# Two hybrid blocks on one core: eight more products on constants in the second block's layer norms, and the decay gate's four products in four row groups

## The reference, cut to what matters

```python
for l in range(DEPTH):                                   # DEPTH = 2
    y = hybrid_mixer(x, positions, w_in[l], gla_w_gate[l], gla_b_gate[l], ...)
    x = layer_norm(DN_ALPHA * x + y, ln1_g[l], ln1_b[l])
    y = conv_ffn(x, w_up[l], conv_w[l], conv_b[l], w_down[l])
    x = layer_norm(DN_ALPHA * x + y, ln2_g[l], ln2_b[l])
```

```python
gate_logits = g_lr @ gla_w_gate + gla_b_gate             # [512, 16] @ [16, 512] + [512]
log_a = jax.nn.log_sigmoid(gate_logits.astype(F32)) / GLA_TAU
```

## Time and profile before

| | us |
|---|---|
| median of 3 runs | 3383.66 |
| lowest, highest | 3381.45, 3383.67 |
| the profiled execution's own time | 3377.7 |
| its span, first to last instruction | 3375.9 |
| TensorE busy in it | 3314.1 (98%) |
| DVE, ACT, POOL busy | 1539.0, 1370.6, 1460.8 |

### The profile page before, as it was taken

The page is one execution under the profiler, slowest core; times in us unless marked ns, Lnnn a source line. Parts: engine busy times, 40 slices in busy tenths (PEclk is TensorE's granted clock), DMA queues, the critical chain, the costliest instruction groups (busy, mean ns, idle before and its releaser), DMA issues. The chain is left out here.

```text
span 3375.9 us, 45275 instructions
## 1 busy us (share of the span) xinstructions
PE 3314.1 (98%) x16644; PEld 2745.6 (81%) x16644; DVE 1539.0 (46%) x2470; ACT 1370.6 (41%) x1976; POOL 1460.8 (43%) x1100
## 2 busy tenths in 40 slices
PE   8999999999999999999999999999989999999998
PEld 6888888887788888887778878888878788788887
DVE  5523232225614442225872446544488524464445
ACT  4534232223635342223364453433444734343333
POOL 4434444444333544444433345445544333444443
PEclk9999999999999999999999999999999999999999
DMA  4222222222222222222212222222222121222221
GB/s 142 84 75 77 98 98 90 99 100 95 81 76 75 101 99 100 89 98 94 84 63 75 76 80 99 88 99 99 100 76 88 56 83 63 88 87 100 99 100 63
DMA packets 43819, 298.60 MB, mean 88 GB/s; under 512 B 4816, under 2 KB 5456, under 8 KB 8592
## 3 DMA queue, kind: packets, MB, share of 16 engines
q1 hardware_dynamic: 41696, 291.52, 24.3%
q10 hardware_dynamic: 1968, 4.94, 0.5%
HBM read 294.34 MB, written 2.10 MB: 88 GB/s over the span
## 5 line engine op out<-in xcount | busy, mean ns | idle before, releaser
L340 POOL TENSOR_TENSOR w_lo<-w_raw,w_hi 128x512 fp32r<-128x512 f32 x1048 | 1392.1, 1360 | 1857.1 <-ACT w_hi L1181 1857.1
L504 PE MATMUL ps<-x_hi,w_hi 128*128 128x512 f32 (+1 forms) x2448 | 966.2, 395 | 7.2 <-POOL w_lo L340 4.9
L506 PE MATMUL ps<-x_hi,w_lo 128*128 128x512 f32 (+1 forms) x2448 | 952.0, 389 | 0.0
L505 PE MATMUL ps<-x_lo,w_hi 128*128 128x512 f32 (+1 forms) x2448 | 951.1, 389 | 0.0
L1181 ACT ACTIVATE w_hi<-w_raw 128x1024 fp32r<-128x1024 f32 x524 | 523.9, 1049 | 486.9 <-PE ps L506 374.4
L504 PEld LDWEIGHTS ps<-x_hi,w_hi 128*128 128x128 f32 x2448 | 459.7, 188 | 111.5 <-issue 8.9
L506 PEld LDWEIGHTS ps<-x_hi,w_lo 128*128 128x128 f32 x2448 | 459.5, 188 | 96.1
L505 PEld LDWEIGHTS ps<-x_lo,w_hi 128*128 128x128 f32 x2448 | 460.0, 188 | 93.6 <-issue 2.4
L504 PE MATMUL ps<-y_hi,w_hi 128*128 128x512 f32 x1056 | 411.6, 390 | 2.7 <-POOL w_lo L340 1.9
L505 PE MATMUL ps<-y_lo,w_hi 128*128 128x512 f32 x1056 | 410.9, 389 | 0.0
L506 PE MATMUL ps<-y_hi,w_lo 128*128 128x512 f32 x1056 | 410.9, 389 | 0.0
(11 more groups left out here) (255 smaller groups left out, 3866.3 us busy)
## 6 DMA issues: line engine op xcount, KB each, us to landing
w_raw<-stream SPq DMA_DIRECT2D x274, 1024.0 KB, 4.8
x<-x_t SPq DMA_DIRECT2D x4, 512.0 KB, 5.9
rotary<-rot ACTq DMA_DIRECT2D x4, 512.0 KB, 3.6
y_t<-x SPq DMA_DIRECT2D x8, 256.0 KB, 2.0
ct<-consts ACTq DMA_DIRECT2D x2, 770.0 KB, 5.3
arena<-pos ACTq DMA_DIRECT2D x2, 256.0 KB, 2.6
vec<-vectors ACTq DMA_DIRECT2D x4, 116.0 KB, 2.0
ct<-consts ACTq DMA_DIRECT2D x1, 128.0 KB, 3.6
```

Of the source, the lines that this page charges most:

```text
L340: ins = nc.gpsimd.tensor_tensor(low(c)[:, o:o + S], RAW[:, c % 2, o:o + S], high(c)[:, o:o + S].bitcast(F32), ALU.subtract)
L504: pe.matmul(ps, wh, xh, start=(k == 0), stop=False)
L505: pe.matmul(ps, wh, xl, start=False, stop=False)
L506: return pe.matmul(ps, wl, xh, start=False, stop=last)
```

## The change

Eight products on constants are issued at the head of `layer_sums`, in all four norms, on `bank + 2` (bank 6 in `ln1`, bank 2 in `ln2`). The gate's weights and its input stand four times, in partitions 0 to 31, 32 to 63, 64 to 95 and 96 to 127, the input with 128 tokens in each; product n takes partitions 32n to 32n+31. `WG`'s DMA grows from 64 KB to 256 KB. DVE's fill becomes one of 128x128, and its copy four copies of 16x128.

```diff
-        WG = sb("w_gate", [32, S])
+        WG = sb("w_gate", [P, S])
...
             def layer_sums(t, l, which, bank):
 
+                keep_clock(bank + 2, 4)
                 T.after((t, l, which + "_sq_sum"), bank_reader[bank + 3], own=False)
                 token_columns(TMP[:, 1, :], bank + 3, P, True, False)
...
                 for n in range(NB):
                     T.after((t, l, "s_read") if n < 2 else (t, l, "pt_read"), own=False)
-                    T.done(pe.matmul(PS[:, 4 + n, :], AR[0:32, 13, n * P:(n + 1) * P], WG[:, :],
+                    T.done(pe.matmul(PS[:, 4 + n, :], AR[32 * n:32 * n + 32, 13, 0:P], WG[32 * n:32 * n + 32, :],
                                      start=True, stop=True), t, l, "gate", n)
...
                 V.after()
-                V.done(dve.memset(AR[0:32, 13, :], 1.0))
+                V.done(dve.memset(AR[:, 13, 0:P], 1.0))
                 V.after()
-                V.done(dve.tensor_copy(AR[0:16, 13, :], AR[64:80, 18, :]), t, l, "glr")
+                for n in range(NB):
+                    V.done(dve.tensor_copy(AR[32 * n:32 * n + 16, 13, 0:P], AR[64:80, 18, n * P:(n + 1) * P]), t, l, "glr")
                 V.after()
...
-    wgate = np.zeros((DEPTH, 32, S), np.float32)
+    wgate = np.zeros((DEPTH, NB, 32, S), np.float32)
     for l in range(DEPTH):
-        wgate[l, 0:GLA_RANK] = i["gla_w_gate_2"][l]
-        wgate[l, GLA_RANK] = i["gla_b_gate_2"][l]
+        wgate[l, :, 0:GLA_RANK] = i["gla_w_gate_2"][l]
+        wgate[l, :, GLA_RANK] = i["gla_b_gate_2"][l]
```

More of the change, by code:

```diff
@@ L2357 @@
     consts, rot = _constants()
-    wgate = np.zeros((DEPTH, 32, S), np.float32)
+    wgate = np.zeros((DEPTH, NB, 32, S), np.float32)
     for l in range(DEPTH):
-        wgate[l, 0:GLA_RANK] = i["gla_w_gate_2"][l]
-        wgate[l, GLA_RANK] = i["gla_b_gate_2"][l]
+        wgate[l, :, 0:GLA_RANK] = i["gla_w_gate_2"][l]
+        wgate[l, :, GLA_RANK] = i["gla_b_gate_2"][l]
     arrays = {
         "stream": _stream(i), "x_t": np.ascontiguousarray(i["x"][0].T), "consts": consts, "rot": rot,
-        "vectors": _vectors(i), "w_gate_in": wgate,
+        "vectors": _vectors(i), "w_gate_in": wgate.reshape(DEPTH, P, S),
         "pos": np.ascontiguousarray(np.broadcast_to(i["positions_2"].astype(np.int32), (P, S))),
```

## The result

Fourteen runs of each kernel: 3386.62 us median after (3383.61 to 3391.01), 3382.14 us before (3377.97 to 3386.32). The ratio is 1.0014, 95% interval 1.0007 to 1.0020: some 5 us slower, inside the 0.2% that was set as the bound of "no change".

What follows compares the result with a forecast made beforehand. TensorE, busy 3314.1 of 3375.9 us, was taken as the bound. Norms +9.53 less gate 3.58 gave +5.95 us, so 3383.65 against the profiled execution, plus 5.96 to the runs' median: 3389.6 us, range 3386.9 to 3393.9.

Steps and rivals of the forecast that it cites:

- The norms: Eight filler products ahead of each of four layer norms delay TensorE: 2 x 2.37 + 1.34 + 3.45 = 9.53 us lost.
- The last norm's term: ln2 of layer 1: no wait at its head, so the fillers cost their full 3.45 us.
- the other three terms: Filler cost at ln1 of layer 0 (2.37 us), ln1 of layer 1 (2.37) and ln2 of layer 0 (1.34).
- all the cover there is: At the norms' heads, TensorE's listed waits, 2.3 and 0.7 us, were claimed as the only place to hide fillers.
- The bound of 10.8 us: Upper bound on the norms' loss: full filler price less the listed waits, 4 x 3.45 - 3.0 us.
- The gate: Four gate products in four row groups take 1.06 us instead of 3.63; 3.58 us gained over two layers.
- the cap: At wa panel 1, la ahead of L1933 in DVE's order limits the gate's gain to 1.79 of 2.57 us a layer.
- Rival 1: At L1061 the row groups do not overlap: whole 3.58 us gain lost, +9.53 us, 3393.2 us; chance 0.10.
- The copies: DVE's fill and four copies ahead of the ropes: 0.85 us for 0.90, effect put at 0, -0.1 to +0.5 us.
- I keep that distance: Base of the forecast: 5.96 us, median of shown runs above the profiled execution, added to 3383.65 us.
- Rival 3: A stretch at granted clock 0.50 falls elsewhere: +1.7 us more, +7.65, 3391.3 us, slower; chance 0.08.
- Rival 2: Fillers at ln2 of layer 0 remove a half-clock stretch, up to 1.7 us: +4.25, 3387.9 us; chance 0.17.

Runs made afterwards that it cites:

- e9: The kernel before, unchanged, run once more as a single execution for its trace: 3383.88 us.

## Why the prediction was right and where it was wrong

**The norms: right.** 9.53 us forecast, 9.39 measured in each of two traces and 9.34 in the third. That nothing behind absorbs the delay came out as read. The last norm's term was 0.1 too high, since the first group gets shorter behind the fillers; the other three terms had that in them. One sentence ahead of the terms was wrong, and they did not rest on it: the 3.0 us of listed waits are not "all the cover there is". Of 13.8 us of fillers 4.4 were covered. In `ln1` of layer 0 it is 1.10 us where the list has 0.57, because a listed wait begins at the end of a record, which lies behind the start of the next product in a dense stretch (0.39 us against 0.23 in the earlier trace rows), and because the groups stand 0.89 us apart when nothing holds them. The bound of 10.8 us, worked out from the list, lay 1.4 us above what was lost for this reason.

**The gate: right, and the cap with it.** 1.07 us for the four, -1.73 per layer for a forecast of -1.79. Undoing the cap by DVE's order gave the whole 2.53. Rival 1, products one behind the other, is refuted. The Trainium skill, "TensorE: Matmul & The Clock Gate", on packing small matmuls, had 3.07x; here it was 3.63 / 1.07 = 3.4x.

**The copies: the term of the sum that was mis-sized.** I put 0.17 us for each, the time of a fill, and 0 for the stage. Four took 1.36 us. DVE's timeline of the changed kernel, layer 1:

```profile
2512.34 0.17 DVE L2187 MEMSET arena<- 128x128 f32 x1
2512.54 1.36 DVE L2190 COPY arena<-arena 16x128 f32<-16x128 f32 x4
```

Behind them DVE is 0.54 us later than before against the rest of the program, in both layers, the upper end that I had named. But this lateness is not what TensorE paid for: matched one to one, DVE is level again 6 us later (at the shuffle that stood at 2513.62 before), and DVE, ACT, POOL and TensorE all are as late as each other up to 2627.3 (but for one pause of 0.35 us at 2538.6, made good within 2 us). There a pause of DVE is new. Before, timelines of DVE and POOL:

```profile
2627.35 0.17 DVE L1904 RECIPROCAL stats<-stats 128x2 f32<-128x2 f32 x1
2627.55 0.69 DVE L1907 TENSOR_TENSOR scratch<-scratch,stats 128x512 f32<-128x512 f32 x1
```

```profile
2627.57 1.82 POOL L340 TENSOR_TENSOR w_lo<-w_raw,w_hi 128x512 fp32r<-128x512 f32 x1
```

And after:

```profile
2633.88 0.17 DVE L1905 RECIPROCAL stats<-stats 128x2 f32<-128x2 f32 x1 [0.46 <-ACT arena L1248]
2634.07 1.49 DVE L1908 TENSOR_TENSOR scratch<-scratch,stats 128x512 f32<-128x512 f32 x1
```

```profile
2633.74 1.27 POOL L340 TENSOR_TENSOR w_lo<-w_raw,w_hi 128x512 fp32r<-128x512 f32 x1
```

The reciprocal begins 0.35 us later than everything around it, so POOL's instruction is the first to begin, where it had been DVE's by 0.02 us. DVE's then takes 1.49 us and not 0.69, POOL's 1.27 and not 1.82, and TensorE's product at L689 waits 0.6 us for DVE. The pause stands at this reciprocal in all seven traces in which the four copies are ahead of the ropes, and in none of the seven others. The instruction of ACT that the row names had not become later. With all engines level just ahead of it, it seems to go with which instructions stand ahead in DVE's program and not with how long they take; that is argued, and what makes the pause isn't shown.

**The step that failed: "The median of the runs shown is 5.96 us above that execution, and I keep that distance: 3383.66".** Three runs stood for a distribution 10 us wide; the median of 14 was 3382.14, and later series gave 3381.82 and 3381.39. This alone is 1.5 us of the 3.0 us by which 3389.6 was too high, and more than the 0.3 us by which the range was missed: its low end was worked out as 3383.66 + 3.2, and from 3382.14 it would have been 3385.3. I had the spread in hand (3381.45 to 3383.67, and a profiled run at 3377.7, outside it) and gave it about 1 us.

The other 1.5 us can't be assigned with certainty. The difference itself came out as 4.5 us by the medians, then 7.6 us on another chip, with intervals of 2.4 to 6.8 and 3.4 to 9.5, and 5.95 lies in both. So does the 6.62 us of work that the traces show: with the 0.69 us that the sum lacked the forecast would have been further off, so one miss hid part of the other by luck. The first series lies 2.1 us under the work. Rival 3, a stretch that falls elsewhere, is what all three traces of the changed kernel have, near 1992, for its 1.7 us (1.6 measured), and still the time was not its 3391.3: the kernel before has stretches in its timed runs that the one profiled execution did not have (mean granted clock 0.9965 to 0.9969 in three series, 0.998 there). Rival 2's clock gain may be real in kind: falls behind `ln2` were seen in 3 traces of 8 without fillers and in none of 6 with them, which is few. At 3 of 8 and 1.65 us it would be worth 0.6 us in the mean, half of the 1.34 us that the fillers cost there, and nothing for the three other norms, behind none of which a fall was ever seen. The fillers alone at +10.8 us, 7 to 14 by the interval, for 9.3 us of work, show no time given back. The clock gain that I did not think of belongs to the gate: 3 of 10 falls gone at 1.6 us each, about 1.0 us for two layers, in the direction of the 4.5 us that the gate alone gained for 2.75 us of work and of its higher granted clock. That this is the whole of it isn't shown.

## What to carry to other kernels

Products on constants ahead of a wait cost at most what they exceed the wait by (3.45 us into 1.85 cost 1.34); sized to it (eight records into 1.85 us) they cost nothing, sixteen into no wait cost 3.35 us. When a product gets shorter, look for the next engine's program order before its durations: one swap on DVE was worth 0.8 us a layer. When a step appears far behind an edit, match every engine's instructions between the two before calling it lateness: the 0.54 us of the copies was gone 115 us before the 0.69 us appeared. And take the base of a forecast from as many runs as the measurement will have, or widen the range by the spread of the runs shown, the profiled one among them.

## What was not expected of the hardware

Half clock came behind 3.6 us of busy TensorE with a quarter of its rows in use, without any idle time ahead (2695.24 to 2698.9 in e9), and, of a second kind, behind waits of 1.8 us. The Trainium skill, "TensorE: Matmul & The Clock Gate", in the table on what matters for kernels, asks for work on TensorE without long idle gaps; the second kind of fall agrees in that it came behind a gap, though behind a shorter one than that row names, and the first came with no gap at all. The measurement decides: gaps are not the whole of it. What sets the stretch ahead of the first kind apart from dense work is the rows in use, but that they are the cause is argued, from 3 falls at 10 gates of one kind and none at 18 of the other. Packing the gate's products into four row groups also took that stretch of thin work away.

Four float32 products of 32 rows started 7 ns apart, all first passes together and all second passes 0.53 us later, though each of them waited for a step and counted one. Small DVE copies over partitions, 16x128, took 0.61 us for the first of the four and 0.22 for each of the others, while a copy of 16x512 had taken 0.42.
